# Placing TensorE's operands at 64 and 128 modulo 512 bytes in a two-block transformer kernel

## What is computed

```python
def swiglu(x, w_gate, w_up, w_down):
    return (jax.nn.silu(x @ w_gate) * (x @ w_up)) @ w_down

for l in range(DEPTH_2):
    x = x + 0.5 * swiglu(rms_norm(x, norm_ffn1[l]), ffn1_w_gate[l], ffn1_w_up[l], ffn1_w_down[l])
    x = x + hybrid_mixer(rms_norm(x, norm_mix[l]), ...)
    x = x + 0.5 * swiglu(rms_norm(x, norm_ffn2[l]), ffn2_w_gate[l], ffn2_w_up[l], ffn2_w_down[l])
```

## The kernel before

| tensor | start modulo 512, before |
|---|---|
| `x`, `xg_hi`, `xg_lo`, `w_raw`, `w_hi`, `w_lo`, `ws_raw`, `ws_hi`, `ws_lo`, `up_raw`, `x_scratch` | 128 |
| `hid`, `heads`, `y` of both blocks, `route_parts`, `worked`, `val` | 384 |
| `xs_hi`, `xs_lo` | 64 |
| tiles of tokens and hidden values in the expert stage | 128 |
| `in_hi`, `in_lo`, chunk c | 128 + 64c, and 64 more where only the 512 tokens are read |

## Time and profile before

### The profile page before, as it was taken

The page is one execution under the profiler, slowest core; times in us unless marked ns, Lnnn a source line. Parts: engine busy times, 40 slices in busy tenths (PEclk is TensorE's granted clock), DMA queues, the critical chain, the costliest instruction groups (busy, mean ns, idle before and its releaser), DMA issues. The chain is left out here.

```text
span 2533.8 us, 38482 instructions
## 1 busy us (share of the span) xinstructions
PE 2439.9 (96%) x15217; PEld 2119.3 (84%) x15217; DVE 1702.0 (67%) x2316; ACT 1129.6 (45%) x1586; POOL 423.0 (17%) x450
## 2 busy tenths in 40 slices
PE   7997997999999999999999999999999999999998
PEld 6886776889897878778898989999888887899996
DVE  5455996668686444567686878787844446687776
ACT  5343884335353233546353454444412255544443
POOL 0002111712112400012121102111050001121110
PEclk9997998999999999999999999999999999999999
DMA  4126995246554321135564546565432213465652
GB/s 145 59 67 206 391 413 204 83 134 167 149 124 132 107 75 62 57 97 157 144 163 143 130 127 170 143 165 145 121 110 90 69 43 92 131 161 148 164 141 77
DMA packets 120714, 348.69 MB, mean 138 GB/s; under 512 B 16067, under 2 KB 21075, under 8 KB 120275
## 3 DMA queue, kind: packets, MB, share of 16 engines
q1 hardware_dynamic: 81634, 245.48, 29.1%
q0 software_dynamic: 38032, 98.06, 16.6%
q10 hardware_dynamic: 864, 2.62, 0.3%
HBM read 331.95 MB, written 12.58 MB: 136 GB/s over the span
## 5 line engine op out<-in xcount | busy, mean ns | idle before, releaser
L522 DVE TENSOR_TENSOR w_lo<-w_raw,w_hi 128x1024 fp32r<-128x1024 f32 (+2 forms) x353 | 421.4, 1194 | 140.7 <-ACT w_hi L517 139.7
L517 ACT ACTIVATE w_hi<-w_raw 128x1024 fp32r<-128x1024 f32 (+2 forms) x353 | 352.6, 1004 | 349.7 <-PE bank_l L566 328.3
L566 PE MATMUL bank_l<-xg_hi,w_hi 128*128 128x512 f32 x872 | 345.9, 397 | 4.9 <-DVE xg_lo L629 4.8
L566 PE MATMUL bank_l<-xg_hi,w_lo 128*128 128x512 f32 x872 | 339.6, 389 | 0.0
L566 PE MATMUL bank_l<-xg_lo,w_hi 128*128 128x512 f32 x872 | 339.6, 389 | 0.0
L566 PE MATMUL bank_l<-hid_hi_ff,w_hi 128*128 128x512 f32 x704 | 275.3, 391 | 4.9 <-DVE hid_lo_ff L654 4.6
L566 PE MATMUL bank_l<-hid_lo_ff,w_hi 128*128 128x512 f32 x704 | 274.2, 389 | 0.0
L566 PE MATMUL bank_l<-hid_hi_ff,w_lo 128*128 128x512 f32 x704 | 274.0, 389 | 0.0
L2045 ACT ACTIVATE ws_hi<-ws_raw 128x1024 fp32r<-128x1024 f32 x142 | 150.6, 1061 | 274.2 <-DVE ws_raw L2167 134.5
L1905 PE MATMUL bank_s<-xs_hi,ws_hi 128*128 128x256 f32 x852 | 237.6, 279 | 2.5 <-DVE ws_lo L2134 2.0
L1905 PE MATMUL bank_s<-xs_lo,ws_hi 128*128 128x256 f32 x852 | 235.7, 277 | 0.0
(11 more groups left out here) (460 smaller groups left out, 5692.7 us busy)
## 6 DMA issues: line engine op xcount, KB each, us to landing
ws_raw<-in_ff_up POOLq DMA_DIRECT2D x213, 256.0 KB, 4.1
w_raw<-in_ff_gate SPq DMA_DIRECT2D x88, 512.0 KB, 3.9
expert_raw<-in_experts SPq DMA_DIRECT2D x81, 512.0 KB, 19.0
w_raw<-in_in SPq DMA_DIRECT2D x80, 512.0 KB, 3.5
w_raw<-in_ff_down SPq DMA_DIRECT2D x64, 512.0 KB, 4.4
ws_raw<-in_ff_gate POOLq DMA_DIRECT2D x71, 256.0 KB, 5.5
up_raw<-in_ff_up SPq DMA_DIRECT2D x71, 256.0 KB, 2.9
w_raw<-in_out SPq DMA_DIRECT2D x24, 512.0 KB, 3.5
```

Source lines behind the costliest of these rows:

```text
L517: act.activation(split_memory(i)[0], split_part(i), ACT.Copy).then_inc(*panel_hi.done(i))
L522: dve.tensor_tensor(lo, split_part(i), hi.bitcast(F32), ALU.subtract).then_inc(*panel_lo.done(i))
L566: done = pe.matmul(dst, w[:, c * cols:(c + 1) * cols], moving, start=c == 0 and n == 0, stop=c == kc - 1 and n == 2)
```

## The change

It changes where tensors lie, and nothing else of the work: no instruction, wait or transfer is added or taken away.

- A filler of 448 bytes ahead of `x` brings `x`, `xg`, `w_raw` and `w_hi` to 64 modulo 512.
- The ring entries of `w_hi` and `w_lo` become 512 bytes longer, so both lie at 64. Panels of block products are put 64 bytes further in (`SHIFT`), at 128.
- `strict`, `router_bias`, `warm`, `suffix` and `minus` move into space that is free later; fillers are resized. `hid`, `heads` and the second block's `y` come to 64, the first block's `y` to 320, `route_parts` and the expert stage's tiles to 320, `ws` stays at 128 and `xs` at 64.
- The rotation's scratch tensor `turning` goes; POOL uses `first_rstd` in its place.

| operands (moving / stationary), modulo 512 | before | after |
|---|---|---|
| block products, `xg` / `w` or `ws` | 128 / 128 | 64 / 128 |
| block products, `xs` / `w` or `ws` | 64 / 128 | 64 / 128 |
| full length, `xg` / `w` | 128 / 128 | 64 / 64 |
| full length, `hid`, `heads`, second `y` / `w` | 384 / 128 | 64 / 64 |
| full length, first `y` / `w` | 384 / 128 | 320 / 64 |
| router, `xg` / `route_parts` | 128 / 384 | 64 / 320 |
| experts, `w` / tile | 128 / 128 | 64 / 320 |
| opening, chunk c, 512 columns | 192+64c / 128 | 128+64c / 64 |

```diff
+SHIFT = 16
+        sb(stack, "before_x", [P, 112])
         x = sb(stack, "x", [P, DC, T])
-        w_hi = sb(stack, "w_hi", [P, SPLIT, PANEL], F32R)
-        w_lo = sb(stack, "w_lo", [P, SPLIT, PANEL], F32R)
+        w_hi = sb(stack, "w_hi", [P, SPLIT, PANEL + 128], F32R)
+        w_lo = sb(stack, "w_lo", [P, SPLIT, PANEL + 128], F32R)
-        router_bias = sb(stack, "router_bias", [P, ROUTES])
-        warm = sb(stack, "warm", [P, 1])
-        strict = sb(stack, "strict", [P, P])
-        suffix = sb(stack, "suffix", [P, P])
-        minus = sb(stack, "minus", [P, P])
+            sb(phase, "before_y1", [P, 32])
             y1_hi = sb(phase, "y1_hi", [P, DC, T], F32R)
             route_parts = sb(phase, "route_parts", [P, 2, PANEL], F32R)
+            strict = sb(phase, "strict", [P, P])
+            router_bias = sb(phase, "router_bias", [P, ROUTES])
+            warm = sb(phase, "warm", [P, 1])
+            suffix = sb(phase, "suffix", [P, P])
+            minus = sb(phase, "minus", [P, P])
-        sb(stack, "before_spent", [P, 40])
+        sb(stack, "before_spent", [P, 8])
-            sb(phase, "before_xs", [P, 48])
             xs_hi = sb(phase, "xs_hi", [P, 4, DC // 2, T // 2], F32R)
             xs_lo = sb(phase, "xs_lo", [P, 4, DC // 2, T // 2], F32R)
-            sb(phase, "behind_xs", [P, 16])
+            sb(phase, "before_ws", [P, SHIFT])
             ws_hi = sb(phase, "ws_hi", [P, 4, PANEL // 2], F32R)
-                    turning = sb(rope, "turning", [P, T])
             if slot_of_panel[i][0] == "up":
-                return w_hi[:, ring_of[i], PANEL // 2:], w_lo[:, ring_of[i], PANEL // 2:]
+                at = slice(PANEL // 2 + SHIFT, PANEL + SHIFT)
+                return w_hi[:, ring_of[i], at], w_lo[:, ring_of[i], at]
+            if by_seven(i):
+                at = slice(SHIFT, PANEL + SHIFT)
+                return w_hi[:, ring_of[i], at], w_lo[:, ring_of[i], at]
-                pool.tensor_tensor(turning[:, :], qk[:, i, :], cos[:, :], ALU.mult).then_inc(
+                pool.tensor_tensor(first_rstd[:, :], qk[:, i, :], cos[:, :], ALU.mult).then_inc(
```

More of the change, by code:

```diff
@@ L2871, in mixer_2_pool @@
                 pool.wait_ge(*swapped[i % 2].upto((l, i, 3)))
-                dst, a, b = qk[:, i, :], turning[:, :], rot[:, i % 2, :]
+                dst, a, b = qk[:, i, :], first_rstd[:, :], rot[:, i % 2, :]
                 if i not in (6, 7):
```

## The result

| | before | after |
|---|---|---|
| time, median of 20 runs each on one chip | 2536.05 us | 2541.48 us |
| ratio, 95% interval | | 1.0022 (1.0016 to 1.0029) |
| span of the profiled execution | 2533.8 us | 2538.8 us |
| granted clock, mean share | 0.988 | 0.989 |

The changed kernel is 5.4 us slower; I had forecast 3.5 us less, and the range ended at 2541. Lines of the code behind the change are five higher: L1910 is L1905 of before, L571 is L566, L2139 is L2134, L2204 is L2199, L659 is L654.

The account below looks back on a forecast made before the run. PE looked busy 96%, but DVE's 10.15 us a pair against PE's 9.76 was taken to end groups of eight. Gains of 0.7 (eights), 2.8 (sixes) and 0 (fives) made -3.5 us: 2531.5 us, range 2514 to 2541.

Parts of the forecast that it names:

- Block products fall to 113.3 ns: Block products on `xg`, PE: 64/128 makes them as cheap as `xs` ones, 0.24 us a pair, 17.0 us of PE time.
- the slower rival: Full-length products on PE: steps settle at 233 ns, 6.7 ns more, giving 2569 us; chance 0.08.
- Groups of eight end with DVE's chain, groups of six have 0.70 us to give: Block product groups: those of eight gain 0.18 us each, 0.7 in all; those of six 0.70 each, 2.8 in all.
- PE's waits for `ws_lo` above 5 us: Sign in the profile after: PE's wait for `ws_lo`, 2.0 us before, grows to more than 5.
- Full length, experts, router, DVE, ACT, POOL: nothing: Everything beside the block products: 0 us; full-length steps stay 226.7 ns, with ends of -37.6 and +37.6 us.
- The place is not the cause: Rival on block products: chunk distance of `xg` and `xs` may make the 6.7 ns; nothing changes, 2535 us; chance 0.13.
- The whole PE saving arrives: Rival on block products: DVE's period shrinks with PE's, all 17.0 us reach the end, 2518 us; chance 0.11.

Follow-up runs that it names:

- the right entry: Changed kernel with one 256-column matmul at 128/128 added ahead of each group's first block product: 2535.28 us, 0.9996 of before.
- the streams: Matmuls run alone, the kernel's computation left out, at chosen operand places behind chosen matmuls; 256 columns at 64/128 stepped 113.3 or 117.8 ns.
- the exchange on DVE: DVE's L2198 put ahead of the rest of the first weight sums: changed kernel 2538.96 us (1.0012); kernel before 2532.06 (0.9978), again 2531.25 (0.9990).
- DVE's hole closed too: Changed kernel with one matmul at 128/128 ahead of each group and DVE's L2198 moved ahead: 2527.33 us (0.9964), again 2524.88 us (0.9963).

## Why the prediction was wrong

*Block products fall to 113.3 ns.* This step failed. I took a step for a property of two places, because all `xs` products in the earlier trace rows had it. In fact it is a property of the places and of what ran ahead: 113.3 ns where one matmul at 128/128 was put ahead of the group, 117.8 without. The value of the term was +0.13 us a pair instead of -0.24 in groups of eight and six: the 36 matmuls on `xg` gave back 0.06 us (4.24 for 4.30) and the 48 on `xs`, which the sum held fixed, took 0.19 more (5.65 for 5.46). The trace of before had the second step in it. In the last pair of its first group of eight PE is held up ahead of S1 T1, where it needs `ws_lo`: the first matmul of that product, at 647.51, starts 0.31 us behind the one ahead of it instead of 0.11. The records go to 281 ns there, and the two products behind it start here:

```profile
649.03 0.28 PE L1905 MATMUL bank_s<-xs_hi,w_hi 128*128 128x256 f32 x1
...
650.45 0.28 PE L1905 MATMUL bank_t<-xg_hi,ws_hi 128*128 128x256 f32 x1
```

A22 T4, at 64/128, takes 650.45 - 649.03 = 1.42 us where it takes 1.36 in the earlier trace rows. The records of all products of that form, instead of one pair, would have shown it, and with it the question what a group is entered with.

*The range and the slower rival.* I looked for a loss in the full-length products only. The mechanism that came was in the very term I had taken for the sure gain, and I had bounded that term from below by 17 us and not from above; its upper bound, all 84 matmuls at the dearest step of the trace, 120 ns, would have been 56 pairs x (10.08 - 9.76) = 18 us.

*Groups of eight end with DVE's chain, groups of six have 0.70 us to give.* Right where 113.3 ns runs. With three extra matmuls a group a group of eight with its down products takes 122.05 us, of which 0.35 are the extra ones: 121.70 against 121.94 in the two undisturbed groups of before, 0.24 less (predicted 0.18). A group of six takes 92.17 - 0.35 = 91.82 against 92.67, 0.85 less (predicted 0.70). With one extra matmul the sum of my terms, -3.5 us, and 11 x 0.12 us for the matmuls make -2.2; measured were -1.0 us (-3.5 to +1.5). That agrees with the sum and with no change as well; the lengths of the groups are what speaks for the sum. One point was off: DVE had not used up its lead in every group of eight, two of the four ended at PE's own 78.07 us.

*PE's waits for `ws_lo` above 5 us.* 5.5 us came, but in the groups of five alone; with the right entry it is 8.1, and 6.7 for `hid_lo`.

*Full length, experts, router, DVE, ACT, POOL: nothing.* Right, as far as the traces tell. The dense streams at 64/64 and 320/64 step 226.7 ns; the expert stage's streams at 64/320 do at best, 226.7 to 227.1, as they did at 128/128, and many there are slower in both kernels; DVE's rest of the weight sums takes 1224 ns on average as before. The step of 233 ns of my slower rival exists, at 64/128 in the streams, and the opening, whose distances keep their series, steps near it before and after. No product on `xg`, `hid` or `y` has that distance at full length.

*The place is not the cause.* The Trainium skill ("TensorE: Matmul & The Clock Gate", Part 2, step ①) gives moving operand and weight load independent read ports, by which places would not matter. The streams don't agree with that conclusion for time: same instructions, no other engine, and 120.0 ns at 64/64 against 113.3 or 117.8 at 64/128. Whether the ports take part in it no run here shows. The 215.7 ns that the same page of the Trainium skill gives for 512 columns ("Wait — 56ns, not 53.3ns?") were reached in no place tried; 226.7 was the least.

*The whole PE saving arrives.* No: at 113.3 ns PE meets DVE's 10.15 us. With the exchange on DVE in both, the places with the right entry are worth 6.4 us, still far from 17.0.

## What to carry to other kernels

The step of back-to-back fp32r matmuls depends on the places of the two operands, and at some pairs of places it can have two steady values, set by what ran ahead. So read the step of a form over the whole span, by its records, before taking it as the price of a layout; if it has two values, ask what stands ahead of each, and look whether a change takes that away. And when one engine is made faster beside another that is nearly as late, measure both together: here the placement gave +5.4 us alone, -1.0 with the entry mended, which isn't clear of noise, and -9.6 with DVE's hole closed too, of which 3.2 are the exchange's own.

## What the runs showed of the hardware that I had not expected

One matmul of 256 columns, 0.12 us, settles how fast the next 420 run: 113.3 or 117.8 ns each, with no idle time in either case, and it lasts over changes of tensors as long as the distance stays. At 128/128 two in a row settle it the other way, three as one does; 30 do as three do. A short wait can turn it both ways: in the group of five of the changed kernel to 113.3, in the kernel with one extra matmul in three places to 117.8. In one of them PE had waited 0.20 us at 1321.04, and the next two products took 1.41 and 1.42 us:

```profile
1321.04 0.38 PE L1910 MATMUL bank_s<-xs_hi,ws_hi 128*128 128x256 f32 x1 [0.20 <-DVE ws_lo L2143]
...
1322.56 0.28 PE L1910 MATMUL bank_s<-xs_hi,w_hi 128*128 128x256 f32 x1
...
1323.97 0.28 PE L1910 MATMUL bank_t<-xg_hi,ws_hi 128*128 128x256 f32 x1
1325.39 0.28 PE L1910 MATMUL bank_t<-xg_hi,w_hi 128*128 128x256 f32 x1
```

What in the chip keeps the two states is open: the runs show which entry leads to which step, and no record tells why. It is open too how a wait leads to one or the other. Its length alone doesn't tell: in the kernel with one extra matmul PE waited 0.35 us at 648.57 and its records stayed at 276 ns, and 0.36 us at 2258.34 and they went to 281.
